# Scatter of the expert outputs through a 0/1 matrix in the rounded matmul format, with the router weight applied while the outputs are evacuated

## What is computed

```python
def swiglu(h, w_gate, w_up, w_down):
    return (jax.nn.silu(h @ w_gate) * (h @ w_up)) @ w_down

def moe_swiglu(h, w_router, w_gate, w_up, w_down):
    logits = (h @ w_router).astype(jnp.float32)
    top_val, top_idx = lax.top_k(logits, TOP_K)
    top_w = jax.nn.softmax(top_val, axis=-1)
    comb = jnp.sum(jax.nn.one_hot(top_idx, N_EXPERTS) * top_w[..., None], axis=-2)
    out = jnp.zeros_like(h)
    for e in range(N_EXPERTS):
        out = out + comb[..., e:e + 1] * swiglu(h, w_gate[e], w_up[e], w_down[e])
    return out
```

## Time and profile before

| | us |
|---|---|
| median of 3 runs (2246.82 to 2252.52) | 2248.12 |
| the profiled execution | 2247.36 |
| its span in the profile | 2245.6 |
| PE busy | 2013.2 (90%) |
| DVE busy | 1376.7 (61%) |
| ACT busy | 946.3 (42%) |

### The profile page before, as it was taken

The page is one execution under the profiler, slowest core; times in us unless marked ns, Lnnn a source line. Parts: engine busy times, 40 slices in busy tenths (PEclk is TensorE's granted clock), DMA queues, the critical chain, the costliest instruction groups (busy, mean ns, idle before and its releaser), DMA issues.

```text
span 2245.6 us, 21290 instructions
## 1 busy us (share of the span) xinstructions
PE 2013.2 (90%) x8429; PEld 1457.2 (65%) x8429; DVE 1376.7 (61%) x1669; ACT 946.3 (42%) x1091; POOL 255.5 (11%) x225
## 2 busy tenths in 40 slices
PE   4899996879799978999958796999999999999996
PEld 4455763746478854557537364788888878788885
DVE  2686437520355526864474203789898888989895
ACT  3121134121344331210341123567676676767674
POOL 6661000200000045600002000000000000000000
PEclk9999998989899989999979997899999999999998
DMA  5323332014544243233210234699899988989892
GB/s 183 117 90 113 113 113 75 1 38 150 169 168 169 80 154 112 75 112 140 93 68 1 70 133 153 226 337 368 322 359 331 361 330 323 356 310 368 322 366 96
DMA packets 202049, 419.03 MB, mean 187 GB/s; under 512 B 8040, under 2 KB 47312, under 8 KB 201952
## 3 DMA queue, kind: packets, MB, share of 16 engines
q1 hardware_dynamic: 196464, 414.20, 51.3%
q10 hardware_dynamic: 4816, 2.34, 0.4%
q0 software_dynamic: 672, 1.17, 0.3%
HBM read 416.64 MB, written 1.05 MB: 186 GB/s over the span
## 4 chain that ended last, share of the span: by engine, by line
PE 79%; DVE 11%; ACT 5%; issue 2%; POOL 2%; ACTq 1%; DVEq 0%
PE bank L1881 19%; PE bank L2233 12%; PE bank L2235 12%; PE bank L2234 12%; PE bank L1874 7%; DVE split_e L1261 2%; PE bank L2330 1%; DVE phase L1444 1%; PE bank L1950 1%; PE bank L2342 1%; PE bank L1937 1%; POOL ring L712 1%; PE bank L1905 1%; PE bank L2110 1%; PE bank L2108 1%
## 5 line engine op out<-in xcount | busy, mean ns | idle before, releaser
L1261 DVE TENSOR_TENSOR split_e<-ring,split_e 128x2048 fp32r<-128x2048 f32 x264 | 599.9, 2288 | 61.7 <-ACT split_e L815 61.5
L815 ACT ACTIVATE split_e<-ring 128x2048 fp32r<-128x2048 f32 x264 | 503.6, 1918 | 185.7 <-PE bank L2235 185.7
L1881 PE MATMUL bank<-ring,hT 128*128 128x512 f32 x768 | 344.4, 605 | 1.7 <-ACT hT L1041 1.7
L2233 PE MATMUL bank<-split_e,fx_e 128*128 128x512 f32 x704 | 283.3, 402 | 2.0 <-DVE fx_e L1751 2.0
L2235 PE MATMUL bank<-split_e,fx_e 128*128 128x512 f32 x704 | 275.5, 391 | 0.0
L2234 PE MATMUL bank<-split_e,fx_e 128*128 128x512 f32 x704 | 274.8, 390 | 0.0
L1881 PEld LDWEIGHTS bank<-ring,hT 128*128 128x128 f32 x768 | 149.8, 196 | 176.5 <-issue 171.8
L2233 PEld LDWEIGHTS bank<-split_e,fx_e 128*128 128x128 f32 x704 | 132.5, 188 | 29.5 <-DVE fx_e L1751 2.2
L2235 PEld LDWEIGHTS bank<-split_e,fx_e 128*128 128x128 f32 x704 | 132.6, 188 | 28.8
L2234 PEld LDWEIGHTS bank<-split_e,fx_e 128*128 128x128 f32 x704 | 132.9, 189 | 27.7 <-issue 1.7
L2233 PE MATMUL bank<-split_e,f_actT_e 128*128 128x512 f32 x352 | 141.5, 402 | 8.5 <-DVE f_actT_e L1759 8.5
(11 more groups left out here) (416 smaller groups left out, 2915.7 us busy)
## 6 DMA issues: line engine op xcount, KB each, us to landing
ring<-in_moe_w_gate SPq DMA_DIRECT2D x40, 2048.0 KB, 9.9
ring<-in_moe_w_up SPq DMA_DIRECT2D x40, 2048.0 KB, 9.5
ring<-in_moe_w_down SPq DMA_DIRECT2D x40, 2048.0 KB, 9.1
ring<-in_w_in SPq DMA_DIRECT2D x28, 2048.0 KB, 7.9
ring<-in_ffn_w_gate SPq DMA_DIRECT2D x11, 1024.0 KB, 5.4
ring<-in_ffn_w_up SPq DMA_DIRECT2D x11, 1024.0 KB, 8.0
ring<-in_ffn_w_down SPq DMA_DIRECT2D x11, 1024.0 KB, 8.8
ring<-in_ssm_w_glu SPq DMA_DIRECT2D x8, 1024.0 KB, 6.2
```

What stands on the lines that cost most here:

```text
L815: nc.scalar.activation(split_e[j % NBUF][:, HI, :], ring[:, s * PIECE + i * HGRP:s * PIECE + (i + 1) * HGRP], ACT.Copy).then_inc(split_hi, 1)
L1261: V.tensor_tensor(split_e[j % NBUF][:, LO, :], ring[:, s * PIECE + i * HGRP:s * PIECE + (i + 1) * HGRP], split_e[j % NBUF][:, HI, :].bitca ...
L1881: last = mm(B[bank][:, :], src[:, k, t * P:(t + 1) * P], w[:, k, n0:n0 + 512], start=k == 0, stop=k == kt - 1)
L2233: mm(bank, a[HI], w[HI], start=first, stop=False)
```

## The change

- `weight_m` and its DVE function `weight_matrix` go. `turn_weights` transposes `gather_m` itself, so that `scatter_m` is a matrix of zeros and ones, stored in the rounded format.
- Behind the two transposes PE makes two float32 matmuls of 8 columns, `gather_m` by `comb` (the router's weights by expert), which give each slot its weights; ACT copies column e into `slot_w` (128x1), one more small instruction in chunk 3.
- `take_y` on ACT multiplies by `slot_w` and writes the HI half of y in the rounded format. It signals after each of its two copies (`ye_hi`).
- The new function `rest_of_y` on DVE writes the LO half, y \* slot_w - HI, in two instructions of 128x512, in chunk 1 between gate group 1 and up group 0 of DVE's list. It signals `ye_ready`.
- `scatter` makes two matmuls in the rounded format for each of its four pieces (HI, then LO).
- `gather_matrix` of the next expert moves from chunk 2 to chunk 3, since `gather_m` is now also read by `turn_weights`.

```diff
@@ -285,9 +285,12 @@
         gather_m = rf.take(NT, P)
-        weight_m = rf.take(NT, P)
-        scatter_m = rf.take(NT * P)
-        y_e = rf.take(D)
+        slot_w = rf.take(8)
+        rf.take(-rf.at % 8 + 8)
+        scatter_at = rf.at
+        rf.take(NT * P)
+        y_at = rf.at
+        rf.take(2, D)
 
@@ -304,6 +307,9 @@
         f_actT_e = over("f_actT_e", [P, 2, FW // P, P], phase_at + 4 * (op_at + 2 * KD * P))
+        scatter_m = over("scatter_m", [P, NT * P], phase_at + 4 * scatter_at)
+        y_e = over("y_e", [P, 2, D], phase_at + 4 * y_at)
+        assert scatter_at % 8 == 0 and y_at % 8 == 0
         mf_th, mf_a, mf_act = (phase[:, i * FW:(i + 1) * FW] for i in range(3))
@@ -360,8 +366,8 @@
         gain_in, h_gain, place_ready = (sem(n) for n in ("gain_in", "h_gain", "place_ready"))
-        gm_ready, wm_ready, he_ps, sm_ps, sm_ready, ye_ready, sc_ps, sc_used = (
-            sem(n) for n in ("gm_ready", "wm_ready", "he_ps", "sm_ps", "sm_ready", "ye_ready", "sc_ps",
+        gm_ready, ye_hi, he_ps, sm_ps, sm_ready, ye_ready, sc_ps, sc_used = (
+            sem(n) for n in ("gm_ready", "ye_hi", "he_ps", "sm_ps", "sm_ready", "ye_ready", "sc_ps",
                              "sc_used"))
@@ -1165,9 +1171,10 @@
                         act.wait_ge(split_used, g0 + group_at["d", n, NFULL, 0] + 1)
+                        act.wait_ge(sm_ready, 2 * (n + 1))
                         for b in range(2):
-                            last = nc.scalar.activation(y_e[:, b * 512:(b + 1) * 512], B[4 + b][:, :], ACT.Copy)
-                        last.then_inc(ye_ready, 1)
+                            nc.scalar.activation(y_e[:, HI, b * 512:(b + 1) * 512], B[4 + b][:, :], ACT.Copy,
+                                                 scale=slot_w[:, 0:1]).then_inc(ye_hi, 1)
 
@@ -1201,7 +1208,8 @@
                                     act.wait_ge(sm_ps, n + 1)
-                                    nc.scalar.activation(scatter_m, B[6][:, 0:2 * P], ACT.Copy).then_inc(sm_ready, 1)
+                                    nc.scalar.activation(slot_w[:, 0:1], B[6][:, 2 * P + e:2 * P + e + 1], ACT.Copy).then_inc(sm_ready, 1)
+                                    nc.scalar.activation(scatter_m[:, :], B[6][:, 0:2 * P], ACT.Copy).then_inc(sm_ready, 1)
                                 if c == 1 and e > 0:
@@ -1721,20 +1729,20 @@
                             dve.wait_ge(he_ps, n)
+                            dve.wait_ge(sm_ps, n)
                         e = n % NE
...
 
-                    def weight_matrix(n):
-                        if n > 0:
-                            dve.wait_ge(sm_ps, n)
-                        e = n % NE
-                        for t in range(NT):
-                            last = V.tensor_scalar(weight_m[:, t, :], steps[:, 0:P], place[:, t, e:e + 1],
-                                                   comb[:, t, e:e + 1], ALU.is_equal, ALU.mult)
-                        last.then_inc(wm_ready, 1)
+                    def rest_of_y(n):
+                        for b in range(2):
+                            dve.wait_ge(ye_hi, 2 * n + b + 1)
+                            last = V.scalar_tensor_tensor(y_e[:, LO, b * 512:(b + 1) * 512], B[4 + b][:, :], slot_w[:, 0:1],
+                                                          y_e[:, HI, b * 512:(b + 1) * 512].bitcast(F32),
+                                                          ALU.mult, ALU.subtract)
+                        last.then_inc(ye_ready, 1)
 
@@ -1781,7 +1789,6 @@
 
-                            dve.wait_ge(wm_ready, NE)
                             dve.wait_ge(gm_ready, NE)
@@ -1799,6 +1806,8 @@
                                     times_up(*prev)
+                                if c == 1 and e > 0:
+                                    rest_of_y(n - 1)
                                 if c == 2 and e > 0:
@@ -1816,9 +1825,7 @@
                                     gated(n, c)
-                                if c == 1:
-                                    weight_matrix(n)
-                                if c == 2 and e < NE - 1:
+                                if c == 3 and e < NE - 1:
                                     gather_matrix(n + 1)
@@ -1826,6 +1833,7 @@
                         tail_lo(n, NFULL)
+                        rest_of_y(n)
                         add_scattered(n, range(4))
@@ -2324,7 +2332,7 @@
                         if n % NE:
-                            pe.wait_ge(sm_ready, n)
+                            pe.wait_ge(sm_ready, 2 * n)
                         for k in range(KD):
@@ -2333,22 +2341,28 @@
 
-                        pe.wait_ge(sm_ready, n + 1)
+                        pe.wait_ge(sm_ready, 2 * (n + 1))
                         pe.wait_ge(ye_ready, n + 1)
...
                                 pe.wait_ge(sc_used, 4 * n + (i - 1))
-                            mm(B[6 + i % 2][:, :], scatter_m[:, t * P:(t + 1) * P], y_e[:, n_ * 512:(n_ + 1) * 512],
-                               start=True, stop=True).then_inc(sc_ps, 1)
+                            for a in (HI, LO):
+                                last = mm(B[6 + i % 2][:, :], scatter_m[:, t * P:(t + 1) * P],
+                                          y_e[:, a, n_ * 512:(n_ + 1) * 512], start=a == HI, stop=a == LO)
+                            last.then_inc(sc_ps, 1)
 
...
 
-                        pe.wait_ge(wm_ready, n + 1)
-                        if n > 0:
+                        if n % NE:
                             pe.wait_ge(sc_used, 4 * n)
+                        else:
+                            pe.wait_ge(fx_ready, fx_before(l) + n + 1)
                         for t in range(NT):
-                            last = tr(B[6][:, t * P:(t + 1) * P], weight_m[:, t, :], ident[:, :])
+                            tr(B[6][:, t * P:(t + 1) * P], gather_m[:, t, :], ident[:, :])
+                        for t in range(NT):
+                            last = mm(B[6][:, 2 * P:2 * P + NE], gather_m[:, t, :], comb[:, t, 0:NE], start=t == 0,
+                                      stop=t == NT - 1)
                         last.then_inc(sm_ps, 1)
```

## The result

The changed kernel takes 2255.99 us (median of 7 runs), the kernel before, in the 7 runs beside it, 2246.82: a ratio of 1.0043 with a 95% interval of 1.003 to 1.0056. It is slower, by 9.2 us or 0.4%, and inside the range of 2250 to 2261.

The account below looks back on a forecast made before the run. PE was taken to set the expert stage's pace, if DVE stays ahead. Seven experts at 0.5 + 0.45 us and the first at 0.45 made 7.1 us slower, named as 2255 us, range 2250 to 2261.

Parts of the forecast that it names:

- the lost cover: Seven experts: late adds use up the cheaper scatter's 1.62 us gain, and 0.5 us each is lost.
- the small matmuls: PE, each expert: two added float32 matmuls of 8 columns, four records, cost 0.45 us; other end 0.88.
- DVE's wait for ACT: DVE, chunk 1 behind gate group 1: idle 2.45 us until ACT's first copy of y, everything behind it queued.
- The LO operations: DVE, chunk 1: two 512-column operations from 1630.55, 0.68 each with 0.60 between starts, DVE free at 1631.75.
- Up group 0 late: PE, chunk 1: DVE's split of up group 0 ends at 1634.04, PE wanted it at 1633.73; 0.48 us lost with restart.
- The first add: DVE, start of chunk 2: starts at 1646.75 instead of 1644.20, behind six splits and three small operations without waits.
- PE's wait for the add: PE, ahead of the third scatter: waits 1.48 us for DVE's first add, so chunk 2 begins at 1648.6, not 1648.11.
- The end: Behind the last expert: y 0.75 us later, scatters cheaper by 0.4 each; about 0, between -0.5 and +0.5.
- The slack: Kernel before, start of chunk 2: adds done at 1645.47, said to be 0.9 us before PE wants the third scatter.
- the gain arrives: Rival: adds done by 1646.0, given 1.4 us less on DVE; 1.17 gained an expert, about 8 in all; chance 0.10.
- the new wait lowers the clock: Rival: PE's idle 1.5 us halves its clock, every scatter costs some 3 us more, total 2276; chance 0.03.
- the scatter does not get cheaper: Rival: rounded scatters run at 0.43 us a record, 6.9 instead of 1.8, total 2279 or so; chance 0.02.

Follow-up runs that it names:

- e2: Changed kernel without the two 8-column matmuls in each expert, the slot's weight read from another column; 2255.58 us, ratio to the kernel before 1.0036.
- e1: Changed kernel with DVE's two LO operations of y moved behind the splits of both up groups; 2239.46 us, ratio to the kernel before 0.9964.
- e3: Changed kernel with ACT's two copies of y moved ahead of its split of up group 1; 2245.53 us, ratio to the kernel before 0.9984.
- e6: Kernel before plus only a DVE wait for ACT's copies of y, between gate group 1 and up group 0 of chunk 1; 2255.11 us, ratio 1.0029.
- e4: Changed kernel with the first two adds of chunk 2 moved on DVE ahead of the gate group 1 split; 2246.60 us, ratio to the kernel before 0.9995.
- e5: Changed kernel with the LO half of y left out of the scatter, DVE's LO operations kept; 2256.96 us, ratio to the kernel before 1.0036.

## Why the prediction was right

The forecast was 7.1 us slower, from two prices an expert, 0.5 for the lost cover and 0.45 for the small matmuls; measured are 9.2 in the medians and 8.3 in the stage. Step by step, on the clock of before:

- **DVE's wait for ACT**: foreseen 2.45 us, measured 2.35, seven times. That the first LO starts at 1630.55: 1630.54.
- **The LO operations**: taken as 0.68 with 0.60 between starts. They took 0.746 (1.41 for the two), so DVE was free at 1631.86 and not 1631.75.
- **Up group 0 late**: 0.48 was foreseen, a wait of 0.36 and 0.12 for the restart. The trace's 0.38 counts from the end of the last matmul. From the place where the next could start (1636.08) to 1636.62 it is 0.54, and the one behind it comes 0.07 later than usual: 0.61 in all. In this order the wait for the add takes that up again.
- **The first add**: foreseen at 1646.75, it came at 1646.86. The six splits and three small operations between ran without a gap, at 2.20 and 0.60, as rows 6 had them. The Trainium skill (VectorE: DVE Perf Modes, "The DRAIN you can't avoid") says that the next operation does not start until the pipe is empty, though one that is not held may start earlier. By full durations this add would have come 0.9 later; the trace disagrees, with splits of 2.29 whose successors start after 2.20.
- **PE's wait for the add**: foreseen 1.48, the trace says 1.28, just under the 1.3 to 1.6 that I had named. It counts from the end of the last matmul (0.39 behind its start), while the next could start after 0.227; from there it is 1.44. The third scatter starts at 1647.69 and not 1647.48: 0.11 by the longer LO operations, and 0.10 since PE starts 0.14 behind the end of the add (1649.88 to 1650.02), not 0.05. So chunk 2 begins 0.66 later than before where I had 0.5. This is the term that was sized too low.
- **The small matmuls**: 0.45 foreseen, 0.42 by e2. The start of chunk 3 is where they show.
- **The end**: foreseen between -0.5 and +0.5. From ACT's first copy to the end of the last add it was 5.82 us (2224.01 to 2229.83) and is 6.56 (2232.57 to 2239.13): +0.74, outside those bounds. The work itself came out as foreseen: with the clock at 1.00 the same end takes 5.82 in e1 and e3, the difference 0. What my sum had at nothing is the fall of the clock there.

Together: 7 times 1.0, 0.42 for the first expert and 0.74 at the end, by the clock, are 8.2, the stage's 8.3. The remaining 1 us between stage and median is within what the part ahead of the stage varies by. That the median came within 1 us of the 2255 that I named is in part luck: the difference was 2.1 us above the forecast, and the kernel before measured 1.3 less beside it (2246.82) than the 2248.12 from which I counted.

**The slack was misread.** I called 0.9 us "all the slack there is", from the end of both adds (1645.47) to 1646.39. The third scatter waits for the first add alone (`sc_used` at 4n + 1), done at 1644.20 + 0.68 = 1644.88: 1.5 us ahead. e6 bears this out. Its add came 2.26 later (1646.46 for 1644.20); less 1.5, and with the 0.14 from the end of an add to PE's start, that is 0.9, and PE lost 0.88. With a slack of 0.9 it would have been 1.5. The sum did not use the 0.9, since it went by the times of the first add itself. Two smaller slips changed nothing: the high end adds up to 12.6 and not 12.5, and the waits of PE for DVE also include seven of 0.45 behind L1775 that stood before and after alike.

**The rivals.** That the gain arrives did not happen in this order, and e1, e3 and e4 show at what point it does: as soon as the adds are done before PE wants its third scatter. I had put that point at 1.4 us on DVE. That was too low: it took PE's place from a sum in which up group 0 is late by 0.48. With up group 0 in time PE wants the third scatter at 1645.6 (e1: 1644.29, whose clock is 1.30 behind), and the first add has to come some 2.1 us earlier. e3, with 1.8 less idle, still waits 0.15 by the trace. The gain itself, about 8 us by my rival, is what e1 shows (8.2). That the new wait lowers the clock did not happen at the seven waits of the changed kernel. The windows over one of them and over nearly the whole stage, all seven included, read

```profile
1640.00:1656.00 16.00, 14.72 (x67) 11.68 (x66) 16.00 (x13) 9.28 (x6) 0.00 (x0) 1.00 1.01 381
1430.00:2225.00 795.00, 772.69 (x3590) 634.14 (x3589) 695.47 (x469) 548.57 (x395) 0.00 (x0) 1.00 0.91 333
```

In the first DVE is busy for all of the 16 us and PE idle for 1.28, and the granted clock is 1.00 (2.4 GHz) in both. The rival is not empty, though. Behind PE's new wait of 2.31 us in the last expert the clock fell to 0.50 (1.2 GHz) before the stage was over and cost 0.74 us; behind one of the seven waits of 1.7 us in e5 it fell too and cost 1.6, about half of the 3 that I had priced. The same waits also stand in profiles without a fall (2.31 in e1 and e3, 1.7 six times in e5), so no run here shows what decides it. That the scatter does not get cheaper is refuted by the 0.94 us of its first pair.

The threshold was the weak point, not the mechanism: with a forecast 0.4 us above what can be told from no change, the chances had to be split nearly evenly. The stage alone ended 1.2 us above the forecast, 0.7 of it from the clock at the end and most of the rest from the experts, whose adds lie 1.0 further apart where I had 0.95; the last 1 us of the medians is not explained by the stage.

## What to carry to other kernels

When an instruction that waits is put into an engine's list, price the queue behind it, not the instruction: e6 lost 6.7 us of stage to a wait that added no work. Find the next thing that another engine wants from that queue, read how much ahead it is (here 1.5 us, from the end of the first add to the third scatter), and place the new wait where the engine still has other work to do first. A faster matmul is worth its time only if what it waits for also comes earlier; here the same edit lost 8.3 us or gained 8.2 by where two vector instructions stood. Read the clock in each profile before its length is compared: four of the nine held 0.5 to 1.9 us of it in the stage.

## What was not expected of the hardware

- The four records of the 8-column matmuls came 0.09 us apart, where 32 in a row had taken 0.113 each.
- A scalar_tensor_tensor of 512 columns from PSUM with a pointer scalar and a rounded output took 0.746 us, and the one without a pointer 0.68; the two rows differ in both, and no run parted them. In the profile after, the rounded output alone costs nothing on a tensor_tensor of that size (685 ns at L1767, 684 at L1783), which points at the pointer without showing it.
- A start of PE behind DVE's first add, and behind its split of up group 0, came 0.14 us after DVE's end, against 0.05 behind DVE's LO half of the activations (L1759 before) in chunk 5. Each repeats in all experts; what makes the difference is open.
- The granted clock fell behind one wait of PE of 1.74 us and not behind six of that length (e5), and behind the wait of 2.31 us it fell before the end of the stage in some profiles and behind it in others: the same last instructions took 6.56 or 5.82 us.
- ACT's copy of a single column took 0.15 us, and its next copy started 0.05 behind it.
